# The order in which expert rows are fetched and used: bursts of sixteen of one table, or one row of each table in turn

## The chip, the cores and the metric

The kernel runs on one core of one Trainium2 chip. The time is the device time of one execution in microseconds (us). The engines are TensorE (PE), VectorE (DVE), ScalarE (ACT), GpSimd (POOL) and SyncE (SP); SBUF and PSUM are the two on-chip memories.

## The reference, cut to what matters

A block of four layers (feed-forward halves around an attention of three kinds) is followed by a block of two layers. Each of these two has a mixer and then `peer`, a layer of product keys over 16384 experts. 256 tokens, width 1024, all float32. What the change touches is the last part of `peer`:

```python
def peer(xn, w_q, keys1, keys2, u, v):
    q = (xt @ w_q).reshape(T, PEER_HEADS, 2, PEER_HALF)       # T = 256, 8 heads
    s1 = einsum('thd,nd->thn', q[:, :, 0], keys1)             # 128 keys each
    s2 = einsum('thd,nd->thn', q[:, :, 1], keys2)
    v1, i1 = top_k(s1, 16)
    v2, i2 = top_k(s2, 16)
    sc, ci = top_k(v1[..., :, None] + v2[..., None, :], 16)   # of 256 sums
    experts = i1[ci // 16] * 128 + i2[ci % 16]                # 16 per token and head
    gates = softmax(sc)
    hb = gelu(einsum('tkd,td->tk', u[experts], xt))           # k: 8 heads x 16 picks
    return einsum('tk,tkd->td', gates * hb, v[experts])
```

So every token reads 128 rows of 1024 numbers from table u, takes the dot product of each with its own vector, and sums 128 rows of table v with the coefficients that come out.

## The kernel before

One program runs all six layers. Only the two `peer` phases are touched, and in them only what follows the key scores.

**Steps.** The tokens lie on the 128 partitions, in two halves. A half and a head make a step: `STEPS` = 16 steps, step s being half s // 8 and head s % 8. A step has 16 picks per token (`BURST` = 16), hence 16 rows of u and 16 rows of v. A "row" of the program is one fetch of 128 table rows, one per partition: a tile of 128 x 1024 f32, 524 kB. A layer fetches 512 of them.

**The ring.** The tiles land in a ring of `ROWSLOTS` = 20 slots, 4 in `deep_ring` and 16 in `wide_ring`. `ROWS` is the fetch order, and `row_at` gives row k the slot k % 20. GpSimd issues all the fetches (`gather`, L2605 to L2622; the page records them at L2619) in that order, each an indirect DMA whose row numbers come from `pk_idx`. Before fetch k it waits until row k - 20 has been used, by the semaphore `row_used` (VectorE) or `row_mixed` (PE), whichever `ROW_AFTER` names; before the first u row of a step it also waits for the last pick stage of that step (`pick_stage`).

**The order.** `GATHERS` (L78 to L81) lists bursts: u of step 0, then u of step s and v of step s - 1 for s = 1 to 15, then v of step 15. Each burst is the 16 rows of one table and step.

**Who uses the rows.** VectorE does all dots (`dot`, L2446): the row times the token vectors, which lie in PSUM (`pair[1 + t]`), with the product written back over the row and the sum into `pk_dot`; a second, short instruction reads the sum out. Of the v rows, the eight with even n are added by VectorE (`accumulate`, L2486): `row_sum` (`pair[3]`, PSUM) += coefficient x row; in the last two steps the sum is kept in `resid` (SBUF) instead. The eight with odd n go through PE (L1348, four matmuls each, with a diagonal matrix that ScalarE makes at L1705), which adds them in two other PSUM banks.

**VectorE's own order.** Beside dot n of step s (0 < s < 14) stands pick stage n of step s + 2 (`pick_stage`, L2371 to L2426: 15 stages, two rounds of MAX8, FIND_INDEX8 and MATCH_REPLACE8 on the 128 scores of each half key, the same on the 256 sums, then the arithmetic that makes `pk_idx`). After dot 3 comes `reciprocal` of the step before, after dot 5 its `coefficients` (L2461), which wait for the gelu on ScalarE (L1696). After dot 15 comes `accumulate(s - 1)`, eight instructions in a row:

```python
                    if s > 0:
                        accumulate(s - 1)
                    if s == PK_HEADS:
                        fold(0)
                        add_mixed(0)
```

`fold` adds `row_sum` to `resid` at the end of each half, and `add_mixed` adds PE's sum.

Of the kernel before, what the change touches and what calls it, by code (L numbers as in the profile page):

```python
# [21 lines left out]
ALU = mybir.AluOpType  # L22
# [6 lines left out]
TT = TOK // P  # L29
# [23 lines left out]
PK_HEADS, NKEYS, TOPK = 8, 128, 16  # L53
# [14 lines left out]
BURST = 16  # L68
STEPS = TT * PK_HEADS
PICK_STAGES = 15  # L70


def on_tensor(step):

    return range(1, BURST, 2)


GATHERS = [("u", 0)]  # L78
for _step in range(1, STEPS):
    GATHERS += [("u", _step), ("v", _step - 1)]  # L80
GATHERS += [("v", STEPS - 1)]  # L81


def count_rows():

    used, mixed, after = 0, 0, {}
    for table, step in GATHERS:
        for n in range(BURST):
            if table == "v" and n in on_tensor(step):
                mixed += 1  # L90
                after[table, step, n] = ("row_mixed", mixed)
            else:
                used += 1
                after[table, step, n] = ("row_used", used)
    return used, mixed, after


ROWS_USED, ROWS_MIXED, ROW_AFTER = count_rows()
ROWS = [(table, step, n) for table, step in GATHERS for n in range(BURST)]
ROW_NUMBER = {row: k for k, row in enumerate(ROWS)}  # L100


# [52 lines left out]
def mix_before(turn):  # L155
# [28 lines left out]
                 mixed=4, mixed_read=4),  # L184
# [25 lines left out]
def build(nc, A, out, stop=None):  # L210
    phases = plan()[:stop]
    ctx = ExitStack()
    with ctx:
# [11 lines left out]
        resid = sb("resid", [P, TT, D])  # L225
# [18 lines left out]
        def cut(at, *shape):  # L244
# [111 lines left out]
        pk_coef = sb("pk_coef", [P, 2, BURST])  # L356
# [225 lines left out]
        wide_dmas, n = [], [0] * GSLOTS  # L582
# [1132 lines left out]
        def _(dve):  # L1715
            V = nc.vector
# [713 lines left out]
            def product_keys(ph):  # L2430
                i, at = ph.i, ph.at
# [32 lines left out]

                def accumulate(s):
                    t = s // PK_HEADS
                    for n in range(BURST):
                        if n in on_tensor(s):
                            continue
                        dve.wait_ge(S["coef"], STEPS * i + s + 1)  # L2470
                        row = ROW_NUMBER["v", s, n]
                        await_row(dve, ph, row)
                        coef = pk_coef[:, s % 2, n:n + 1]
                        if s % PK_HEADS == 0 and n == 0:
                            if t == 0:
                                dve.wait_ge(S["key_scores_read"], PK_HEADS * (i + 1))
                            else:
                                dve.wait_ge(S["rows_folded"], TT * i + 1)
                            V.tensor_scalar(row_sum[:], row_at(ph, row), coef, None,
                                            ALU.mult).then_inc(S["row_used"], 1)  # L2480
                            continue
# [3 lines left out]
                        total = resid[:, t] if s >= STEPS - 2 else row_sum[:]  # L2485
                        V.scalar_tensor_tensor(out=total, in0=row_at(ph, row), scalar=coef, in1=total,  # L2486
                                               op0=ALU.mult, op1=ALU.add).then_inc(S["row_used"], 1)
# [28 lines left out]
                split_head(5)  # L2516
                pick(1, 7, PICK_STAGES)
                split_head(6)
                for s in range(STEPS):
                    for n in range(BURST):  # L2520
# [3 lines left out]
                        if s == 0 and n >= BURST // 2:  # L2524
                            pick(2, 2 * n - BURST, min(2 * n - BURST + 2, PICK_STAGES))
                        if 0 < s < STEPS - 2 and n < PICK_STAGES:
                            pick_stage(ph, s + 2, n)
                        if s > 0 and n == 3:
                            reciprocal(s - 1)
                        if s > 0 and n == 5:  # L2530
                            coefficients(s - 1)
                    if s == STEPS - 1:
                        fold(1)
                    if s > 0:
                        accumulate(s - 1)
                    if s == PK_HEADS:
                        fold(0)
                        add_mixed(0)
                reciprocal(STEPS - 1)
                coefficients(STEPS - 1)  # L2540
                accumulate(STEPS - 1)
                add_mixed(1)
            for ph in phases:
                {"norm": norm, "norm_split": norm_split, "norm_final": norm, "ffn": ffn, "sb": stick_breaking,
# [154 lines left out]
```

## Time and profile before

| | |
|---|---|
| median of three runs | 3919.18 us (3918.96 to 3920.58) |
| the profiled execution | 3916.44 us |
| its span | 3914.7 us |
| granted TensorE clock, mean | 0.89 |
| PE, VectorE, ScalarE, GpSimd busy | 76%, 69%, 31%, 27% |
| bytes moved | 940.74 MB, 547.19 of them by GpSimd's queue |

The profile comes from one execution, and its parts are read against that execution's span. In its table of slices each digit is the busy share in tenths; a busy share is not yet a bound, since an engine can be busy in one stage and idle in another. Names such as `wide_ring<-in_peer_u,pk_idx` are out<-in. In a list of waits, "issue" is time in which the engine waited for nothing that the profile shows, and "remote" a wait that it can't put to another engine's instruction. The first `peer` phase fetches rows from about 2227 to 2977 us of the span, the second from about 3155 to 3905.

### The profile page before, as it was taken

The numbers are of one execution on the slowest core, as the hardware profiler recorded it, in microseconds if no ns is written. First come the engines' busy times: TensorE is split into PE (matmuls) and PEld (weight loads), VectorE is DVE, ScalarE is ACT, GpSimd is POOL, SyncE is SP. The second block draws the span as 40 slices with busy tenths as digits, with TensorE's granted clock in tenths as the row PEclk, the third lists the DMA queues.
The fourth block names the chain that finished last, engine by engine and source line by source line (L and its number), as shares of the span: only waits on it lengthen the run. The fifth ranks groups of instructions, "written<-read, shape, count | busy, mean of one in ns | idle before, by whom it ended". The sixth has DMA issues, their size and how long they took to land.

```text
span 3914.7 us, 41030 instructions
## 1 busy us (share of the span) xinstructions
PE 2983.6 (76%) x14720; PEld 2203.6 (56%) x14720; DVE 2697.0 (69%) x4716; ACT 1231.4 (31%) x1807; POOL 1054.3 (27%) x1133
## 2 busy tenths in 40 slices
PE   8999999999999999999999943433338964433344
PEld 7897888968886688897886721111114661111111
DVE  6655676666765667664664687778774587778786
ACT  5444444344442444444442311111111231111110
POOL 2000000000000000000000266666663056666665
PEclk9999999999999999999999967776769987677678
DMA  6634565435554355562563499999998279999998
GB/s 213 207 121 147 192 199 191 169 113 194 190 182 147 129 169 191 193 231 76 167 210 114 152 350 359 362 365 369 366 360 312 81 268 360 365 363 366 364 373 329
DMA packets 413639, 940.74 MB, mean 240 GB/s; under 512 B 24688, under 2 KB 209552, under 8 KB 413472
## 3 DMA queue, kind: packets, MB, share of 16 engines
q0 software_dynamic: 150800, 547.19, 37.0%
q1 hardware_dynamic: 260784, 389.57, 29.6%
q8 instruction: 96, 1.57, 0.2%
q10 hardware_dynamic: 1888, 1.84, 0.1%
q14 instruction: 71, 0.58, 0.0%
HBM read 937.45 MB, written 1.05 MB: 240 GB/s over the span
## 4 chain that ended last, share of the span: by engine, by line
PE 55%; DVE 30%; issue 5%; another core or an unknown queue 4%; DMA 2%; POOL 2%; ACT 1%; DVEq 0%; SPq 0%; POOLq 0%; ACTq 0%
DVE wide_ring L2446 11%; PE pair L937 8%; PE pair L944 8%; DVE pair L2486 7%; PE pair L706 5%; PE pair L708 5%; PE pair L707 5%; PE pair L779 4%; PE pair L942 4%; PE pair L939 4%; PE pair L800 4%; DVE deep_ring L2446 3%; PE pair L787 1%; DMA wide_ring<-in_ffn_w_gate_up 1%
## 5 line engine op out<-in xcount | busy, mean ns | idle before, releaser
L1348 PE MATMUL pair<-wide_ring,arena 128*128 128x512 f32 x816 | 443.7, 691 | 654.0 <-issue 376.6
L1727 DVE TENSOR_TENSOR wide_lo<-wide_ring,wide_hi 128x2048 fp32r<-128x2048 f32 x228 | 522.5, 2292 | 401.1 <-ACT wide_hi L1443 396.7
L1348 PEld LDWEIGHTS pair<-wide_ring,arena 128*128 128x128 f32 x816 | 170.2, 220 | 925.8 <-issue 790.9
L2598 POOL TENSOR_TENSOR small<-small,minus_half 128x2 f32<-128x2 f32 (+2 forms) x29 | 25.2, 869 | 2321.3 <-DVE small L1877 1673.3
L1443 ACT ACTIVATE wide_hi<-wide_ring 128x2048 fp32r<-128x2048 f32 x228 | 434.6, 1911 | 483.6 <-DMA wide_ring<-in_ffn_w_gate_up 323.0
L937 PE MATMUL pair<-x_both,wide_hi 128*128 128x512 f32 x1344 | 533.0, 397 | 1.6 <-DVE wide_lo L1727 1.1
L944 PE MATMUL pair<-x_both,wide_hi 128*128 128x512 f32 x1344 | 531.6, 396 | 0.0
L2446 DVE CUSTOM_DVE_ANT_0 wide_ring<-wide_ring,pair 128x1024 f32<-128x1024 f32 x408 | 490.7, 1210 | 19.3 <-issue 18.8
L2619 POOL DMA_INDIRECT wide_ring<-in_peer_v,pk_idx x408 | 394.5, 967 | 232.4 <-issue 101.1
L2619 POOL DMA_INDIRECT wide_ring<-in_peer_u,pk_idx x408 | 392.5, 962 | 164.2 <-issue 95.2
L942 PE MATMUL pair<-x_both,wide_lo 128*128 128x256 f32 x1344 | 374.2, 278 | 0.0
L939 PE MATMUL pair<-x_both,wide_lo 128*128 128x256 f32 x1344 | 372.8, 277 | 0.0
L1705 ACT ACTIVATE arena<-ident,pk_coef 128x128 f32<-128x128 f32 x256 | 78.3, 388 | 795.0 <-remote 570.0
L942 PEld LDWEIGHTS pair<-x_both,wide_lo 128*128 128x128 f32 x1344 | 252.3, 188 | 61.1
L939 PEld LDWEIGHTS pair<-x_both,wide_lo 128*128 128x128 f32 x1344 | 252.7, 188 | 56.6
L937 PEld LDWEIGHTS pair<-x_both,wide_hi 128*128 128x128 f32 x1344 | 255.1, 190 | 10.1 <-issue 8.0
L1348 PE MATMUL pair<-deep_ring,arena 128*128 128x512 f32 x208 | 114.7, 692 | 180.5 <-issue 80.5
L944 PEld LDWEIGHTS pair<-x_both,wide_hi 128*128 128x128 f32 x1344 | 251.9, 187 | 0.0
L706 PE MATMUL pair<-deep_hi,hid_hi 128*128 128x512 f32 x640 | 249.3, 390 | 0.0
L708 PE MATMUL pair<-deep_hi,hid_lo 128*128 128x512 f32 x640 | 249.0, 389 | 0.0
L707 PE MATMUL pair<-deep_lo,hid_hi 128*128 128x512 f32 x640 | 249.0, 389 | 0.0
L2486 DVE SCALAR_TENSOR_TENSOR pair<-wide_ring,pk_coef,pair 128x1024 f32<-128x1024 f32 x176 | 226.8, 1288 | 30.7 <-issue 6.2
(349 smaller groups left out, 5751.6 us busy)
## 6 DMA issues: line engine op xcount, KB each, us to landing
wide_ring<-in_ffn_w_gate_up SPq DMA_DIRECT2D x174, 1024.0 KB, 9.6
deep_ring<-in_ffn_w_down SPq DMA_DIRECT2D x88, 1024.0 KB, 4.9
wide_ring<-in_sb_w_qkv SPq DMA_DIRECT2D x12, 2048.0 KB, 12.6
wide_ring<-in_w_in SPq DMA_DIRECT2D x12, 2048.0 KB, 9.7
wide_ring<-in_peer_w_q SPq DMA_DIRECT2D x8, 2048.0 KB, 13.9
wide_ring<-in_moba_w_qkv SPq DMA_DIRECT2D x6, 2048.0 KB, 12.3
deep_ring<-in_sb_w_o SPq DMA_DIRECT2D x8, 1024.0 KB, 7.5
deep_ring<-in_w_out SPq DMA_DIRECT2D x8, 1024.0 KB, 7.6
```

The lines of the kernel that those rows point to most:

```text
L706: mm(o, w[0], x[0], start=start, stop=False, skip_group_check=True)
L707: mm(o, w[0], x[1], start=False, stop=False, skip_group_check=True)
L708: return mm(o, w[1], x[0], start=False, stop=stop, skip_group_check=True)
L937: mm(o[:, 0:2 * TOK], hi, both, start=k == 0, stop=False, skip_group_check=True)
L939: mm(o[:, 0:TOK], lo, x_hi[:, k], start=False, stop=False, skip_group_check=True)
L942: mm(o[:, 0:TOK], lo, x_hi[:, k], start=False, stop=False, skip_group_check=True)
L944: ins = mm(o[:, 0:2 * TOK], hi, both, start=False, stop=k == KT - 1, skip_group_check=True)
L1348: ins = mm(acc[t][h][:, :], pk_diag[:, s % 2, k], row_at(ph, row)[:, h * 512:(h + 1) * 512], start=first, stop=last, skip_group_check=True)
L1727: V.tensor_tensor(wide_lo[:, split_at(ph, j)], half_panel(ph, wide_ring[:, slot], j), wide_hi[:, split_at(ph, j)].bitcast(F32), ALU.subtra ...
L2446: V.tensor_tensor_reduce(out=row_at(ph, row), in0=row_at(ph, row), in1=pair[1 + s // PK_HEADS][:], scale=1.0, scalar=0.0, op0=ALU.mult, op ...
L2486: V.scalar_tensor_tensor(out=total, in0=row_at(ph, row), scalar=coef, in1=total, op0=ALU.mult, op1=ALU.add).then_inc(S["row_used"], 1)
L2619: G.indirect_dma_start(row_at(ph, k), None, tables[table], bass.IndirectOffsetOnAxis(ap=pk_idx[:, s, n:n + 1], axis=0)).then_inc(row_in[sl ...
```

## The change

The order of the rows is another. `ROWS` now begins with 24 rows of u (`U_LEAD`), then takes one row of u and one of v in turn, and ends with the 24 rows of v that are left. Beside u row (s + 1, n + 8) stands v row (s, n). VectorE goes through the same list: `accumulate` now handles one row, and it waits by semaphore for the row that VectorE accumulated before it. The pick stages, `reciprocal` and `coefficients` stand beside the same dots as before. `fold` and `add_mixed` are placed by rows of v; `add_mixed(0)` comes three rows of v later than `fold(0)`. PE and ScalarE follow `ROWS` with unchanged code; their instructions and their order are the same as before.

```diff
-GATHERS = [("u", 0)]
-for _step in range(1, STEPS):
-    GATHERS += [("u", _step), ("v", _step - 1)]
-GATHERS += [("v", STEPS - 1)]
+U_LEAD = BURST + BURST // 2
+
+
+def order_of_rows():
+
+    def row(table, k):
+        return table, k // BURST, k % BURST
+    count = STEPS * BURST
+    rows = [row("u", k) for k in range(U_LEAD)]
+    for k in range(count):
+        if k + U_LEAD < count:
+            rows.append(row("u", k + U_LEAD))
+        rows.append(row("v", k))
+    return rows
+
+
+ROWS = order_of_rows()
...
-                def accumulate(s):
+                def accumulate(s, n):
...
-                        dve.wait_ge(S["row_used"], ROWS_USED * i + ROW_AFTER["v", s, n][1] - 1)
-                        if s == STEPS - 2:
-                            dve.wait_ge(S["rows_folded"], TT * (i + 1))
...
+                    before = ("v", s, n - 2) if n > 0 else ("v", s - 1, BURST - 2)
+                    dve.wait_ge(S["row_used"], ROWS_USED * i + ROW_AFTER[before][1])
+                    if s == STEPS - 2 and n == 0:
+                        dve.wait_ge(S["rows_folded"], TT * (i + 1))
...
-                for s in range(STEPS):
-                    for n in range(BURST):
+                for table, s, n in ROWS:
+                    if table == "u":
                         if s == 0 and n == 3:
                             split_head(7)
                         dot(s, n)
...
-                    if s == STEPS - 1:
+                        beside_dot(s, n)
+                        continue
+                    if s == STEPS - 2 and n == 0:
                         fold(1)
-                    if s > 0:
-                        accumulate(s - 1)
-                    if s == PK_HEADS:
+                    if s == STEPS - 2 and n == BURST - 4:
+                        reciprocal(STEPS - 1)
+                    if s == STEPS - 1 and n == 0:
+                        coefficients(STEPS - 1)
+                    if n not in on_tensor(s):
+                        accumulate(s, n)
+                    if s == PK_HEADS - 1 and n == BURST - 1:
                         fold(0)
+                    if s == PK_HEADS and n == 2:
                         add_mixed(0)
-                reciprocal(STEPS - 1)
-                coefficients(STEPS - 1)
-                accumulate(STEPS - 1)
                 add_mixed(1)
```

VectorE before, at the end of a step in mid-layer (ISA is a dot, `ISA pk_dot` the short read of its sum; L2424 and L2426 are the last two pick stages, L2380 is the first of the next):

```order
L2446 ISA wide_ring,pk_dot<-wide_ring,pair 128x1024
L2446 ISA pk_dot 128x1
L2426 SCALAR_TENSOR_TENSOR pk_idx<-pk_e 128x16
L2446 ISA wide_ring,pk_dot<-wide_ring,pair 128x1024
L2446 ISA pk_dot 128x1
L2486 SCALAR_TENSOR_TENSOR pair<-deep_ring,pk_coef,pair 128x1024 x2
L2486 SCALAR_TENSOR_TENSOR pair<-wide_ring,pk_coef,pair 128x1024 x6
L2446 ISA wide_ring,pk_dot<-wide_ring,pair 128x1024
L2446 ISA pk_dot 128x1
L2380 MAX pk_v<-arena 128x8 x2
L2446 ISA wide_ring,pk_dot<-wide_ring,pair 128x1024
```

VectorE after, over the same pick stages (the dot is now L2458, the accumulation L2497):

```order
L2458 ISA wide_ring,pk_dot<-wide_ring,pair 128x1024
L2458 ISA pk_dot 128x1
L2426 CAST pk_ab<-pk_abu 128x32
L2497 SCALAR_TENSOR_TENSOR pair<-wide_ring,pk_coef,pair 128x1024
L2458 ISA wide_ring,pk_dot<-wide_ring,pair 128x1024
L2458 ISA pk_dot 128x1
L2429 TENSOR_TENSOR arena<-pk_ab,iota 128x512
L2458 ISA deep_ring,pk_dot<-deep_ring,pair 128x1024
L2458 ISA pk_dot 128x1
L2433 TENSOR_TENSOR arena<-arena,pk_if 128x512
L2497 SCALAR_TENSOR_TENSOR pair<-deep_ring,pk_coef,pair 128x1024
L2458 ISA deep_ring,pk_dot<-deep_ring,pair 128x1024
```

The eight accumulations that stood together stand one by one, each behind every second dot.

GpSimd before, at the first fetches of the layer that wait for a slot to come free (in brackets the semaphores that a fetch waits for):

```order
L2619 DMA deep_ring<-in_peer_u,pk_idx 128x1024 [waits row_used] x4
L2619 DMA wide_ring<-in_peer_u,pk_idx 128x1024 [waits row_used] x8
L2619 DMA wide_ring<-in_peer_v,pk_idx 128x1024 [waits row_used] x8
L2619 DMA deep_ring<-in_peer_v,pk_idx 128x1024 [waits row_used] x4
L2619 DMA wide_ring<-in_peer_v,pk_idx 128x1024 [waits row_used] x4
L2619 DMA wide_ring<-in_peer_u,pk_idx 128x1024 [waits row_used,pick_stage]
L2619 DMA wide_ring<-in_peer_u,pk_idx 128x1024 [waits row_used] x4
```

GpSimd after, at the same place (the fetch is now L2637):

```order
L2637 DMA deep_ring<-in_peer_u,pk_idx 128x1024 [waits row_used] x4
L2637 DMA wide_ring<-in_peer_u,pk_idx 128x1024 [waits row_used]
L2637 DMA wide_ring<-in_peer_v,pk_idx 128x1024 [waits row_used]
L2637 DMA wide_ring<-in_peer_u,pk_idx 128x1024 [waits row_used]
L2637 DMA wide_ring<-in_peer_v,pk_idx 128x1024 [waits row_used]
L2637 DMA wide_ring<-in_peer_u,pk_idx 128x1024 [waits row_used]
```

Where twelve fetches of u and sixteen of v followed one another, fetches of u and v alternate from the 25th on. The count of instructions on GpSimd, PE and ScalarE is the same; VectorE has 4830 instead of 4844, the 14 fewer being semaphore waits.

## Rows read from the trace of the kernel before

**Rows 1.** The table of slices: three of its lines of tenths in 40 slices.
```profile
PE   8999999999999999999999943433338964433344
DVE  6655676666765667664664687778774587778786
...
DMA  6634565435554355562563499999998279999998
```

**Rows 2.** Windows of ten and eleven steps; columns are named in the first row.
```profile
core 0: us, PE busy (x) PEld busy (x) DVE busy (x) ACT busy (x) POOL busy (x), PEclk, DMA share, GB/s
2343.00:2805.00 462.00, 177.72 (x325) 69.44 (x324) 363.00 (x773) 58.11 (x130) 301.34 (x320) 0.70 0.96 363
3271.00:3778.00 507.00, 191.80 (x356) 74.66 (x355) 399.01 (x850) 63.93 (x143) 331.02 (x352) 0.70 0.96 364
```

**Rows 3.** VectorE's waits in the ten steps: us in total, times, longest us.
```profile
DVE pk_sc L2407 <- remote: 28.8, 7, 6.9
DVE pk_neg L2402 <- remote: 12.2, 8, 2.5
DVE pk_sc L2400 <- remote: 11.6, 4, 6.0
DVE pk_sc L2400 <- issue: 7.1, 2, 6.0
DVE pk_sc L2407 <- issue: 6.5, 2, 5.6
```

**Rows 4.** Lines of GpSimd in the ten steps: busy, mean ns, idle before.
```profile
L2619 POOL DMA_INDIRECT wide_ring<-in_peer_v,pk_idx x128 | 121.1, 946 | 76.3 <-issue 29.6 <-remote 28.0 <-DVE pk_dot L2446 18.7
L2619 POOL DMA_INDIRECT wide_ring<-in_peer_u,pk_idx x128 | 119.9, 936 | 49.1 <-issue 27.3 <-DVE pk_dot L2446 11.0 <-DVE arena L2421 5.5
```

**Rows 5.** Windows inside two steps, in the last burst with dots, and behind it.
```profile
2437.00:2443.00 6.00, 4.66 (x12) 1.82 (x10) 6.00 (x15) 1.77 (x3) 3.91 (x5) 1.00 0.65 199
2443.00:2457.00 14.00, 5.83 (x10) 2.05 (x8) 13.20 (x18) 0.31 (x1) 9.49 (x11) 0.88 0.93 337
2457.00:2483.00 26.00, 8.68 (x16) 3.52 (x16) 16.79 (x46) 3.73 (x9) 16.77 (x18) 0.61 1.03 410
2483.00:2489.00 6.00, 3.28 (x7) 1.17 (x7) 5.72 (x15) 1.77 (x3) 3.75 (x4) 1.00 0.70 222
2489.00:2503.00 14.00, 4.95 (x11) 1.54 (x9) 13.20 (x18) 0.31 (x1) 9.58 (x10) 0.94 0.96 336
2503.00:2528.00 25.00, 7.96 (x13) 3.42 (x14) 16.94 (x46) 3.73 (x9) 16.86 (x18) 0.56 1.02 408
2880.00:2906.00 26.00, 15.26 (x28) 5.84 (x28) 22.77 (x35) 2.75 (x9) 19.59 (x22) 0.73 1.03 409
2934.00:2975.00 41.00, 30.14 (x57) 11.10 (x58) 20.11 (x18) 3.67 (x12) 30.68 (x27) 0.91 0.98 374
```

**Rows 6.** Timeline of VectorE, then of GpSimd, around one wait.
```profile
2528.25 0.43 DVE L2407 MAX8 pk_sc<-arena 128x8 f32<-128x256 f32 x1 [6.94 <-remote]
...
2524.37 0.94 POOL L2619 DMA_INDIRECT deep_ring<-in_peer_v,pk_idx  x1 [0.30 <-issue]
2529.90 0.94 POOL L2619 DMA_INDIRECT deep_ring<-in_peer_v,pk_idx  x1 [4.59 <-DVE pk_dot L2446]
```

**Rows 7.** Lines of VectorE in the ten steps, then one burst from its timeline.
```profile
L2446 DVE CUSTOM_DVE_ANT_0 wide_ring<-wide_ring,pair 128x1024 f32<-128x1024 f32 x128 | 154.8, 1209 | 6.3 <-issue 6.3
L2486 DVE SCALAR_TENSOR_TENSOR pair<-wide_ring,pk_coef,pair 128x1024 f32<-128x1024 f32 x63 | 81.2, 1289 | 8.4
...
2498.32 8.40 DVE L2486 SCALAR_TENSOR_TENSOR pair<-wide_ring,pk_coef,pair 128x1024 f32<-128x1024 f32 x6
```

**Rows 8.** Lines of ScalarE and of PE in the ten steps.
```profile
L1696 ACT ACT_TABLE_LOAD x10 | 12.8, 1283 | 0.2
L1696 ACT ACTIVATE pk_gelu<-pk_dot,small 128x16 f32<-128x16 f32 x10 | 3.1, 308 | 94.4 <-DVE pk_dot L2446 86.4 <-issue 8.0
...
L1348 PE MATMUL pair<-wide_ring,arena 128*128 128x512 f32 x261 | 142.8, 699 | 226.3 <-issue 126.2 <-ACT arena L1705 45.4 <-remote 29.2
```

More of the change, by code:

```diff
@@ L75, in on_tensor @@
     return range(1, BURST, 2)
-GATHERS = [("u", 0)]
-for _step in range(1, STEPS):
-    GATHERS += [("u", _step), ("v", _step - 1)]
-GATHERS += [("v", STEPS - 1)]
+U_LEAD = BURST + BURST // 2
[10 more added lines that the diff above has]
+ROWS = order_of_rows()
 def count_rows():
     used, mixed, after = 0, 0, {}
-    for table, step in GATHERS:
-        for n in range(BURST):
[L89 to L94, printed above, removed]
+    for table, step, n in ROWS:
+        if table == "v" and n in on_tensor(step):
+            mixed += 1
+            after[table, step, n] = ("row_mixed", mixed)
+        else:
+            used += 1
+            after[table, step, n] = ("row_used", used)
     return used, mixed, after
 ROWS_USED, ROWS_MIXED, ROW_AFTER = count_rows()
-ROWS = [(table, step, n) for table, step in GATHERS for n in range(BURST)]
 ROW_NUMBER = {row: k for k, row in enumerate(ROWS)}
@@ L2463, in coefficients @@
                                            ).then_inc(S["coef"], 1)
-                def accumulate(s):
+                def accumulate(s, n):
                     t = s // PK_HEADS
[L2467 to L2481, printed above, removed]
-                        dve.wait_ge(S["row_used"], ROWS_USED * i + ROW_AFTER["v", s, n][1] - 1)
-                        if s == STEPS - 2:
-                            dve.wait_ge(S["rows_folded"], TT * (i + 1))
-                        total = resid[:, t] if s >= STEPS - 2 else row_sum[:]
-                        V.scalar_tensor_tensor(out=total, in0=row_at(ph, row), scalar=coef, in1=total,
-                                               op0=ALU.mult, op1=ALU.add).then_inc(S["row_used"], 1)
@@ new lines, in accumulate @@
+                    dve.wait_ge(S["coef"], STEPS * i + s + 1)
+                    row = ROW_NUMBER["v", s, n]
+                    await_row(dve, ph, row)
+                    coef = pk_coef[:, s % 2, n:n + 1]
+                    if s % PK_HEADS == 0 and n == 0:
+                        if t == 0:
+                            dve.wait_ge(S["key_scores_read"], PK_HEADS * (i + 1))
+                        else:
+                            dve.wait_ge(S["rows_folded"], TT * i + 1)
+                        V.tensor_scalar(row_sum[:], row_at(ph, row), coef, None,
+                                        ALU.mult).then_inc(S["row_used"], 1)
+                        return
@@ new lines, in accumulate @@
+                    before = ("v", s, n - 2) if n > 0 else ("v", s - 1, BURST - 2)
+                    dve.wait_ge(S["row_used"], ROWS_USED * i + ROW_AFTER[before][1])
+                    if s == STEPS - 2 and n == 0:
+                        dve.wait_ge(S["rows_folded"], TT * (i + 1))
+                    total = resid[:, t] if s >= STEPS - 2 else row_sum[:]
+                    V.scalar_tensor_tensor(out=total, in0=row_at(ph, row), scalar=coef, in1=total,
+                                           op0=ALU.mult, op1=ALU.add).then_inc(S["row_used"], 1)
@@ L2518, in product_keys, with beside_dot @@
                 split_head(6)
-                for s in range(STEPS):
-                    for n in range(BURST):
+                def beside_dot(s, n):
+                    if s == 0 and n >= BURST // 2:
+                        pick(2, 2 * n - BURST, min(2 * n - BURST + 2, PICK_STAGES))
+                    if 0 < s < STEPS - 2 and n < PICK_STAGES:
+                        pick_stage(ph, s + 2, n)
+                    if s > 0 and n == 3:
+                        reciprocal(s - 1)
+                    if s > 0 and n == 5:
+                        coefficients(s - 1)
+                for table, s, n in ROWS:
+                    if table == "u":
                         if s == 0 and n == 3:
@@ L2523, in product_keys @@
                         dot(s, n)
[L2524 to L2531, printed above, removed]
-                    if s == STEPS - 1:
-                        fold(1)
-                    if s > 0:
-                        accumulate(s - 1)
-                    if s == PK_HEADS:
+                        beside_dot(s, n)
+                        continue
+                    if s == STEPS - 2 and n == 0:
+                        fold(1)
+                    if s == STEPS - 2 and n == BURST - 4:
[5 more added lines that the diff above has]
+                    if s == PK_HEADS - 1 and n == BURST - 1:
                         fold(0)
+                    if s == PK_HEADS and n == 2:
                         add_mixed(0)
-                reciprocal(STEPS - 1)
-                coefficients(STEPS - 1)
-                accumulate(STEPS - 1)
                 add_mixed(1)
```

## The prediction

> **What bounds the kernel now.** The table of slices comes first [rows 1]. In the two product-key layers (slices 24 to 31 and 33 to 40, of 97.9 us each) the transfer engines' digit is 9 except at the edges and VectorE's mostly 7 or 8, while PE sinks to 3 or 4. So either the fetching or VectorE sets the end there. The two stretches are some 1500 us of the span, and the change touches nothing outside them.
>
> Next, the windows over ten whole steps of the first layer and eleven of the second [rows 2]. I cut them where VectorE resumes after the wait that comes once in each step. 462 by ten and 507 by eleven are **46.1 us per step**. VectorE is busy 363.0 / 10 = 36.3 us of it, the transfer engines 0.96 of it, at 363 GB/s. One row is 128 x 1024 f32, 0.524 MB; a step moves 32 rows, 16.8 MB.
>
> Who waits? VectorE's waits [rows 3] name no transfer at all: it never stands for a row of the tables. They stand at the pick instructions L2400, L2402 and L2407, with no recorded releaser: these first five rows are 66.2 us, 6.6 per step. GpSimd, in turn, waits for slots that VectorE has not freed [rows 4]: `DVE pk_dot` ends 18.7 and 11.0 us of the idle time before its fetches, "remote" 28.0.
>
> The stretches inside two steps show how the two go together [rows 5]. A step has three parts: about 6 us at 199 GB/s, 14 us at 337, and 26 us at 410. The next step repeats it (222, 336, 408). 410 is the ceiling: the last burst without picks runs at 409 as well. At 410 a step would take 16.8 / 0.410 = 40.9 us, so 5.2 us of each step are lost to the first two parts. VectorE is busy 6.0 of 6 and 13.2 of 14 us in them, but only 16.8 of 26 in the fast part. The idle time lies in the last third of the fast part: after dot 7 VectorE stands 6.9 us before MAX8 L2407, whose only wait is for its own, finished predecessor; GpSimd issues three more fetches, finds no free slot and stands for 4.6 us; the transfers drain [rows 6]. That is the 6 us part. I can't name the cause of this stall; I can only say where it comes: after some 17 us of VectorE's work, or 46 of its instructions, at 410 GB/s.
>
> **The change part by part.** It removes no fetch, no dot, no accumulation and no pick: the same 77 recorded VectorE instructions per step (773 in ten [rows 2]), in another order. Cost of the work itself: 0.
>
> *The middle part.* It runs at 337 because slots come free at the pace of a burst of dots. That pace is (36.3 - 8 x 1.289) / 16 = 1.62 us per row [rows 2, 7], the picks included, while a fetch is issued every 0.936 + 0.30 = 1.24 us [rows 4, 6] and lands every 0.524 / 0.410 = 1.28. With one u and one v in turn, VectorE frees two rows with a dot and half an accumulation: 36.3 / 32 = 1.13 us per row, less than 1.24. GpSimd is then never held after the drain, and the 14 us part joins the fast one. The stall stays, and it now comes after 6 + 26 us instead of 46. Such a cycle moves 6 x 199 + 26 x 410 = 11.85 MB, 22.6 rows in 32 us, or 45.3 us per 32 rows: **0.8 us less than 46.1**. The gain is small because the stall with its drain now comes 1.4 times per step. Steps 1 to 13 have picks beside them or just ahead, in two layers: 26 x 0.8 = 21 us.
>
> *The head.* A lead of 24 u rows instead of 32: eight rows leave VectorE's pace of 1.62 for 1.42 (45.3 / 32): 1.6 us per layer, 3 in all.
>
> *The tail.* The last rows are v alone, 32 of them before, 24 now. They run at 374 GB/s, 1.40 us per row [rows 5]; at best eight of them go to 1.28: 1 us per layer, 2 in all.
>
> *The accumulations.* In a burst one takes 8.40 / 6 = 1.40 us against 1.289 busy [rows 7]: 0.11 is the wait for the one ahead. Now a dot stands between. Below, that is 0; above, 0.11 x 8 = 0.9 us per step of VectorE's time, 23 us in all. I take 0, since in the forecast VectorE is not what paces the cycle, and because the pair of waits ahead of the instruction stays.
>
> *The waits that move.* The indices of step s+2 are complete when dot (s, 14) is done. The first fetch that reads them stood 50 places of the fetch order behind that dot and stands 36 behind it now; GpSimd leads by at most 20, so 16 are spare: 0. Between the last dot of a step and its coefficients lie 6 dots and 3 accumulations, about 14 us, where before there were 6 dots and a burst, about 21; the gelu needs its table load and itself, 1.283 + 0.308 us [rows 8]: 0. `add_mixed(0)` may now wait for PE's last row of the half, four matmuls of 0.70 us [rows 8]: 0 to 2.8 once per layer; I take 0. On GpSimd's queue each fetch of v now waits in turn for VectorE and for PE; PE uses a row as it lands, and its slot is asked for 20 places later: 0.
>
> **Sum:** 21 + 3 + 2 = 26 us less. The profiled execution took 3916.4, so 3890 on its own scale. The median of the runs shown is 3919.2, 2.8 above it: **3893**.
>
> **A rule against it.** The row says that 410 GB/s is held for 26 us in each step, and 363 and 364 on the mean in the two layers [rows 2, 5]. The Trainium skill (DMA: Bandwidth & Descriptors, section Bandwidth) says that for transfers from HBM into SBUF the HBM side binds, at about 358 GB/s per core. By that rule there would be nothing to gain, and the time stays 3919. It also gives 425 for a core that streams alone, which is the side on which the 410 lies. The sum goes by the row.
>
> **The rivals.**
> - *Nothing moves* (3919). The mean over a step could be what is limited, in whatever state of the order; 363 and 364 in two layers speak for that, and so does that VectorE does not wait for rows, which means the change mends an unevenness that the ring of 20 already takes up. Against it: the 14 us at 337 follow the pace of the dots. Chance 0.17.
> - *The stalls go* (3784). If they come from dense picks at full rate, spreading the picks over 41 us instead of 26 thins them. VectorE's 36.3 us fit under the 40.9 of the transfers: 5.2 x 26 = 135 us less. In the last burst without picks [rows 5] VectorE is busy 22.8 of 26 us at 409 GB/s, so full rate and a working VectorE go together where there are no picks. Against it: the picks are no fewer per row. Half of that would be 3851. Chance 0.20.
> - *The stall eats VectorE* (slower). If a stall follows each 17 us of VectorE's work at full rate, a cycle of 32 us holds 6.0 + 16.8 = 22.8 us of it. A step then takes 36.3 / 22.8 x 32 = 50.9 us: 4.8 x 26 = 125 us more, 4044. The place is VectorE's queue, at whichever pick stands there. It decides as soon as VectorE is idle for more than 6.4 of 32 us, since 22.6 rows need 25.6; at 7.5 it would be 47.4 us per step and 3953. Now it is idle 9.2 of 26. For the forecast the stall must go by instructions rather than by time: 46 now stand in 16.8 us of work, where all the dense picks are; spread evenly (77 in 36.3) 46 are 21.7 us of work, which leaves 4.3 idle. Chance 0.27.
>
> **How the numbers follow.** Forecast 0.36. Less than 0.2% (8 us) is about what a measurement of this kernel tells from no change. Faster is the forecast and the second rival, 0.56; same is the first, 0.17; slower the third, 0.27. As both signs hold much: the forecast's own range is 3865 (with the 23 us of the accumulations) to 3910. The whole one is 3800 to 3985: it takes in most of the second rival and the nearer half of the third, and leaves out some 0.17.
>
> **What would show it.** Right: windows in mid-layer without a stretch near 337 that lasts 14 us; a mean of 368 to 371 GB/s; waits without a releaser in front of picks, spaced some 32 us. The third rival: the same spacing, a mean under 355, VectorE busy under 0.77. The second: long stretches at 410 and VectorE waiting for rows. The first: 363 again, in whatever pattern. I am wrong altogether if VectorE's busy time per step changes by more than 1 us, or if GpSimd waits for `pick_stage` or `row_mixed`.

## The result, and the profile after

| | before | after |
|---|---|---|
| median | 3919.07 us (3917.55 to 3920.58, 4 runs) | 3894.98 us (3891.74 to 3897.63, 4 runs) |
| the profiled execution | 3916.44 us | 3891.74 us |
| its span | 3914.7 us | 3890.0 us |

The ratio is 0.9942, with a 95% interval of 0.9929 to 0.9955: 24 us faster, where 26 was forecast. One run of the kernel before, among those of the second chip below, took 5490.91 us at a granted clock of 0.549 and not 0.89, and is left out of every comparison. Of the profile after, the lines that answer to [rows 1], and one of PE:

```profile
DVE  6655676666765667664664687878775588778785
...
DMA  6634555535554456462563299999998279999998
...
L1360 PE MATMUL pair<-wide_ring,arena 128*128 128x512 f32 x824 | 548.5, 811 | 558.2 <-DMA wide_ring<-in_peer_v,pk_idx 220.7
```

The line of PE before:

```profile
L1348 PE MATMUL pair<-wide_ring,arena 128*128 128x512 f32 x816 | 443.7, 691 | 654.0 <-issue 376.6
```

In the two product-key layers (slices 24 to 31 and 33 to 40) the digits of the transfers are the same as before; the difference lies inside the steps. So I cut twelve whole steps of each layer, from the first dot of step 2 to the first dot of step 14. The same cut of the kernel before (columns as in [rows 2]):

```profile
2320.40:2875.50 555.10, 211.35 (x384) 82.07 (x384) 435.35 (x929) 69.73 (x156) 362.12 (x385) 0.71 0.96 363
3248.40:3801.50 553.10, 208.06 (x384) 80.81 (x384) 435.21 (x929) 69.74 (x156) 361.09 (x385) 0.70 0.96 365
```

And after:

```profile
core 0: us, PE busy (x) PEld busy (x) DVE busy (x) ACT busy (x) POOL busy (x), PEclk, DMA share, GB/s
2314.20:2852.10 537.90, 260.69 (x382) 92.17 (x383) 427.67 (x928) 69.73 (x156) 362.62 (x383) 0.71 0.97 372
3226.10:3765.50 539.40, 253.71 (x383) 90.27 (x384) 427.15 (x928) 69.74 (x156) 364.11 (x384) 0.72 0.97 372
```

A step took 46.3 and 46.1 us and takes 44.8 and 45.0: 1.3 less, at 372 GB/s instead of 363 and 365. VectorE's busy time fell a little, from 36.3 to 35.6 us per step. In all, the twelve steps gain 17.2 us in the first layer and 13.7 in the second. The rest of each layer is its two ends, steps 0 and 1 and what follows the first dot of step 14; here those of the first layer, before:

```profile
2246.30:2320.40 74.10, 37.12 (x180) 25.57 (x178) 63.76 (x146) 14.60 (x26) 49.19 (x50) 0.72 0.93 338
2875.50:2977.10 101.60, 49.09 (x92) 18.01 (x93) 70.37 (x96) 9.18 (x30) 69.09 (x68) 0.76 0.95 369
```

and after:

```profile
2247.20:2314.20 67.00, 33.69 (x174) 23.85 (x172) 58.41 (x141) 14.18 (x25) 44.96 (x46) 0.73 0.94 342
2852.10:2962.30 110.20, 64.84 (x103) 20.88 (x101) 73.65 (x101) 9.49 (x31) 75.59 (x75) 0.82 0.96 370
```

74.1 + 101.6 = 175.7 became 67.0 + 110.2 = 177.2; in the second layer 175.2 became 178.9. (The first part is shorter and the last longer because the rows of v begin eight rows earlier.) The ends give back 1.5 and 3.7 us. Over both layers that is 30.9 - 5.2 = 25.7 us, against 24.7 by which the spans differ.

VectorE's waits after, which answer to [rows 3] (stretch 2343 to 2780, picks are now L2392 to L2438):

```profile
DVE pk_if L2405 <- remote: 22.6, 6, 4.8
DVE pk_v L2400 <- remote: 12.8, 4, 6.9
DVE pk_v L2400 <- issue: 11.6, 2, 6.9
DVE pk_i L2403 <- remote: 7.7, 3, 3.5
```

Still no transfer is named, and still nothing is recorded that releases these waits. They only stand at other picks, L2400 to L2405 (MAX8 of the second round, FIND_INDEX8, the first CAST). That no transfer is named is weak evidence by itself, since most landings are missing from this trace (last section). But these picks wait by their code for the pick stage before them alone, which had ended, and ahead of all dots VectorE stood for only 10 us in this stretch. And the parts of a step, as in [rows 5]:

```profile
2379.00:2388.00 9.00, 7.45 (x12) 3.00 (x12) 9.00 (x22) 5.50 (x12) 6.86 (x8) 0.74 0.79 263
2388.00:2418.00 30.00, 15.07 (x20) 4.87 (x20) 21.82 (x47) 0.31 (x1) 20.56 (x23) 0.77 1.02 407
2463.00:2475.00 12.00, 3.61 (x5) 1.55 (x6) 11.94 (x29) 3.73 (x9) 8.50 (x10) 0.50 0.84 275
2475.00:2511.00 36.00, 16.95 (x29) 5.84 (x27) 27.89 (x61) 2.08 (x4) 25.76 (x27) 0.83 1.03 411
```

In these two steps 9 and 12 us run at 263 and 275 GB/s, then 30 and 36 us at 407 and 411. The middle part at 337, which was 14 us long, is gone as a part of its own, but the slow part ahead of the fast one is longer than the 6 us that I had put down for it.

### The profile page after: what moved, and what is told of

It reads as the page before. It is cut to its first block, busy times and chain, and to the rows that moved or that the text cites. A ratio compares the mean times of both kernels' runs of the same rounds, so it can differ in the third digit from the quotient of the medians.

```text
span 3890.0 us, 41016 instructions
## 1 busy us (share of the span) xinstructions
PE 3105.2 (80%) x14720; PEld 2225.6 (57%) x14720; DVE 2676.8 (69%) x4716; ACT 1230.8 (32%) x1807; POOL 1063.2 (27%) x1133
## 4 chain that ended last, share of the span: by engine, by line
PE 55%; DVE 27%; issue 8%; another core or an unknown queue 4%; DMA 3%; POOL 1%; ACT 1%; SPq 0%; DVEq 0%; POOLq 0%; ACTq 0%
DVE wide_ring L2458 8%; PE pair L949 8%; PE pair L956 8%; DVE pair L2497 7%; PE pair L718 5%; PE pair L720 5%; PE pair L719 5%; PE pair L791 4%; PE pair L954 4%; PE pair L951 4%; PE pair L812 4%; DVE deep_ring L2458 2%; DMA wide_ring<-in_ffn_w_gate_up 2%; PE pair L799 1%
## 5 line engine op out<-in xcount | busy, mean ns | idle before, releaser
L1360 PE MATMUL pair<-wide_ring,arena 128*128 128x512 f32 x824 | 548.5, 811 | 558.2 <-DMA wide_ring<-in_peer_v,pk_idx 220.7
L1360 PEld LDWEIGHTS pair<-wide_ring,arena 128*128 128x128 f32 x824 | 190.6, 250 | 914.2 <-issue 711.1
L2458 DVE CUSTOM_DVE_ANT_0 wide_ring<-wide_ring,pair 128x1024 f32<-128x1024 f32 x404 | 486.2, 1209 | 13.5 <-issue 12.4
L2637 POOL DMA_INDIRECT wide_ring<-in_peer_u,pk_idx x404 | 396.8, 982 | 188.8 <-issue 112.5
L2637 POOL DMA_INDIRECT wide_ring<-in_peer_v,pk_idx x412 | 398.0, 966 | 176.1 <-issue 118.7
L2497 DVE SCALAR_TENSOR_TENSOR pair<-wide_ring,pk_coef,pair 128x1024 f32<-128x1024 f32 x178 | 227.1, 1276 | 26.5 <-remote 24.8
L1360 PE MATMUL pair<-deep_ring,arena 128*128 128x512 f32 x200 | 135.1, 813 | 121.9 <-DMA deep_ring<-in_peer_v,pk_idx 61.6
```

Source lines behind the costliest of these rows:

```text
L1360: ins = mm(acc[t][h][:, :], pk_diag[:, s % 2, k], row_at(ph, row)[:, h * 512:(h + 1) * 512], start=first, stop=last, skip_group_check=True)
L2458: V.tensor_tensor_reduce(out=row_at(ph, row), in0=row_at(ph, row), in1=pair[1 + s // PK_HEADS][:], scale=1.0, scalar=0.0, op0=ALU.mult, op ...
L2637: G.indirect_dma_start(row_at(ph, k), None, tables[table], bass.IndirectOffsetOnAxis(ap=pk_idx[:, s, n:n + 1], axis=0)).then_inc(row_in[sl ...
```

## The experiments

Two theories stood at the start. **A, VectorE's own time:** it never waits for a row, so a step is its work and its stalls; the gain is that an accumulation no longer stands behind another, where it took 1.40 us and not 1.28. **B, the fetches' pace:** the gain is that slots come free evenly, so that the transfers spend more of the time at 410 GB/s. A third, **C**, was that the shorter lead brings it.

**Turns of four.** One line of `order_of_rows`:

```diff
-    for k in range(count):
-        if k + U_LEAD < count:
-            rows.append(row("u", k + U_LEAD))
-        rows.append(row("v", k))
+    for k in range(0, count, 4):
+        rows += [row("u", j + U_LEAD) for j in range(k, k + 4) if j + U_LEAD < count]
+        rows += [row("v", j) for j in range(k, k + 4)]
```

> The changed order with turns of four: 24 u rows ahead, then four of u and four of v. VectorE then has two accumulations next to one another in each turn, 4 such neighbours per step where the kernel before has 7 and the change none. Theory A (VectorE's own time is the step's time: it never waits for a row, and an accumulation right behind another costs some 0.24 us more than one behind a dot): 4/7 of the 1.3 us per step is lost again, 0.74 x 26 = 19 us, so about 3914 us, and small gaps of VectorE of some 0.6 us per step. Theory B (the fetches' pace: what counted is that slots come free evenly): a ring of 20 evens out four rows, so 3895 within 4.

Measured: 3774.90 us (10 runs), and the kernel before beside it 3775.55 (31 runs): 0.9999 [0.9989, 1.0008].

**Turns of eight**, the same with 8 for 4.

> Turns of eight. 6 neighbouring accumulations per step. Theory A: 6/7 of the gain is lost, 1.1 x 26 = 29 us, capped by the kernel before: about 3919 to 3923. Theory B: eight dots at 1.6 us per row hold GpSimd for a few rows only, so at most a third of the gain is lost: 3895 to 3903.

Measured: 3776.48 us, 1.0000 [0.9991, 1.0010].

**A lead of 32.** `U_LEAD = 2 * BURST`.

> The change with a lead of 32 u rows, as long as before, and then one row of each in turn. Theory A and theory B alike: nothing in mid-layer changes, so 3895 within 5, the ends aside. Theory C (the shorter lead is what brought the gain): 3915 to 3919.

Measured: 3775.20 us, 0.9998 [0.9989, 1.0008].

**Twelve of sixteen v rows on PE.**

```diff
+ON_VECTOR = (0, 4, 8, 12)
...
-    return range(1, BURST, 2)
+    return [n for n in range(BURST) if n not in ON_VECTOR]
```

> The change with 12 of a step's 16 v rows on PE instead of 8; VectorE adds 4. Its work falls by 4 x 1.29 = 5.2 us per step, to 30.5. Theory A: 30.5 plus stalls of 9 is 39.7, under the 40.9 that the transfers need at 410 GB/s, so the step becomes 41 to 42 us and VectorE begins to wait for rows: 28 x 3.5 = about 95 us less, 3800 us (3785 to 3830). Theory B: the stalls still drain the transfers once per 45 us, 3880 to 3895. PE at 2.8 to 3.2 us per row needs 34 to 38 us per step; if it is held, 3850 or more.

Measured: 3775.62 us, 1.0001 [0.9992, 1.0011].

All four expectations missed, under every theory: on this chip the kernel before itself takes 3775.55 us, 144 less than in the runs of the result. Twelve steps of the kernel with turns of four show why (this row and the two below it in the columns of [rows 2]):

```profile
2306.60:2792.40 485.80, 276.27 (x373) 105.74 (x374) 430.12 (x929) 69.72 (x156) 364.58 (x386) 0.72 1.03 409
```

with a lead of 32:

```profile
2299.50:2780.20 480.70, 267.29 (x371) 85.02 (x372) 431.44 (x929) 70.04 (x157) 361.41 (x383) 0.77 1.03 408
```

and with twelve v rows on PE:

```profile
2305.20:2793.30 488.10, 327.11 (x563) 120.27 (x562) 377.41 (x881) 84.08 (x205) 365.30 (x388) 0.85 1.03 409
```

408 to 409 GB/s from end to end, 40.1 to 40.7 us per step. VectorE's busy time in the last of the three is 377 us instead of 430, and the kernel's time is the same. The two largest groups of VectorE's waits with turns of four, in the stretch 2350 to 2700:

```profile
DVE wide_ring L2457 <- DMA wide_ring<-in_peer_u,pk_idx: 23.6, 24, 1.3
DVE pair L2496 <- DMA wide_ring<-in_peer_v,pk_idx: 10.2, 16, 1.3
```

Now transfers end them, and there is no wait without a releaser at a pick. The stalls are not there, and the transfers' 1.28 us per row set the time in all the orders tried. So this group tells nothing of A and B where the stalls are; it shows what the kernels cost where they are not.

**The two kernels themselves, and two loads on VectorE**, on a second chip. (Each group of runs was on one chip at one time, with the kernel before beside it, so the chip and the occasion are not told apart. Which chip the result was taken on is not known.)

> The kernel before, unchanged, for a profile beside the other experiments: in the runs of the first experiments it took 3775.6 us, not 3919. Theory S (VectorE's stalls without a releaser are a condition of the chip or of the run, not of the order, and without them the transfers' 1.28 us per row is the bound): 3775, 409 to 410 GB/s throughout mid-layer, 40.9 us per step, no waits without a releaser at the picks. If the stalls are there: 3919.

Measured: 3927.72 us (10 runs), the kernel before beside it 3927.00. The stalls are there:

```profile
2320.70:2878.10 557.40, 210.40 (x384) 81.11 (x384) 435.25 (x928) 69.82 (x156) 363.36 (x385) 0.70 0.96 361
```

> The changed kernel, unchanged, likewise. Theory S: where the kernel before takes 3775 this one does too, within 0.1%, with VectorE waiting for rows; where it takes 3919 this one takes 3895.

Measured: 3900.88 us (4 runs), 0.9930 [0.9913, 0.9946], 26 us less: the result holds here too.

```profile
2314.10:2857.10 543.00, 267.49 (x384) 93.10 (x384) 428.75 (x928) 69.74 (x156) 364.02 (x385) 0.68 0.98 371
3236.70:3779.50 542.80, 257.58 (x385) 90.34 (x384) 429.30 (x928) 69.75 (x156) 362.62 (x384) 0.71 0.98 370
```

45.2 us per step against 46.5, close to the 44.9 and 46.2 of the result.

**More instructions on VectorE:**

```diff
+                    for q in range(2):
+                        V.tensor_copy(spare[:, 2 * n + q:2 * n + q + 1], minus_half[:, 0:1])
```

> The change with two more instructions of 128x1 behind each dot, on a tile that nothing reads: 32 per step (77 to 109), about 0.07 us each, 2.2 us of VectorE's time. Without stalls: VectorE needs 38 of 40.9 us, the transfers bound, no change from the changed kernel. With stalls: theory N (a stall comes after so many VectorE instructions at full rate): stalls grow by 109/77, 9 to 12.7 us per step, and with the 2.2 the step becomes 51 us: 150 us more than the changed kernel. Theory T (it comes after so much time): 2.2 us per step, 60 us more.

Measured: 3916.84 us (4 runs), 0.9968 [0.9952, 0.9983], 16 more than the changed kernel. Both expectations, 150 and 60 us more, are far too high.

```profile
2322.20:2866.70 544.50, 256.85 (x384) 90.78 (x384) 455.70 (x1313) 69.68 (x157) 363.81 (x384) 0.72 0.98 370
3247.20:3795.50 548.30, 266.40 (x388) 92.33 (x386) 455.51 (x1314) 69.73 (x156) 364.15 (x385) 0.70 0.98 369
```

VectorE is busy 455.6 us instead of 429, 2.2 more per step, and the step is 0.1 and 0.5 us longer. Theory A asks for the whole 2.2. VectorE's idle time shrank instead, from 9.5 to 7.4 us per step in the first layer, and it came in many short waits: in the stretch 2343 to 2780 none is longer than 2.0 us, where the changed kernel on this chip has waits of 6.6. So the idle time does not grow with the number of instructions either.

**Fewer.** This kernel leaves out the picks of steps 3 to 15; they fetch again the rows that step 2 picked:

```diff
+                if s > 2:
+                    if n < PICK_STAGES - 1:
+                        return
...
+                    V.scalar_tensor_tensor(out=pk_idx[:, s], in0=pk_e[:, 0], scalar=float(NKEYS),
+                                           in1=pk_e[:, 1], op0=ALU.mult, op1=ALU.add
+                                           ).then_inc(S["pick_stage"], PICK_STAGES)
```

> The change without the pick stages of steps 3 to 15: those steps fetch the rows that step 2 picked, and their gates are left as they are, so this part of the computation is left out. VectorE's work falls by some 9 us per step, its instructions from 77 to about 43. Without stalls: the transfers bound, so the time stays that of the changed kernel within 0.2%, which would show that VectorE's work has no part in it. With stalls: 41 us per step and 3790 if the stalls need the picks, 3850 or more if they don't.

Measured: 3885.62 us (2 runs), 0.9893 [0.9873, 0.9913], 15 less than the changed kernel: over 3850, as expected if the stalls don't need the picks. That the same table rows are read again is a second difference, which no run takes apart.

```profile
2306.80:2835.30 528.50, 289.96 (x377) 91.09 (x376) 357.25 (x521) 70.13 (x157) 351.96 (x375) 0.71 0.97 373
```

VectorE's busy time is 357 us, 6.0 less per step, and the step is 1.2 less. In both directions a microsecond of VectorE's work is worth 0.05 to 0.2 us of a step. Over the whole kernel it is 0.2 and 0.1: 73 us more of VectorE's work cost 16 us, and 153 less gained 15. **Theory A falls.**

When does a stall come? Here are stretches, picked by eye, from where the transfers reach 410 GB/s to where VectorE first stops. In the kernel before, from the trace that the result was compared with:

```profile
2458.00:2472.00 14.00, 0.00 (x0) 0.00 (x0) 13.58 (x38) 0.00 (x0) 10.50 (x12) 0.50 1.03 413
2505.00:2521.00 16.00, 0.96 (x1) 0.50 (x2) 14.99 (x44) 1.85 (x7) 12.04 (x14) 0.50 1.02 412
2544.00:2562.00 18.00, 0.00 (x0) 0.00 (x0) 16.56 (x37) 0.00 (x0) 13.42 (x16) 0.64 1.02 409
```

in the changed one, from the trace of the result:

```profile
2475.00:2498.00 23.00, 13.41 (x25) 4.67 (x23) 23.00 (x49) 2.08 (x4) 17.51 (x19) 0.91 1.03 412
2524.00:2545.00 21.00, 10.17 (x17) 3.19 (x16) 20.72 (x42) 0.31 (x1) 16.12 (x17) 0.82 1.03 411
2390.00:2406.00 16.00, 7.27 (x11) 2.34 (x10) 16.00 (x33) 0.31 (x1) 12.08 (x13) 0.84 1.03 412
```

with more instructions, on the second chip:

```profile
2529.00:2545.00 16.00, 9.58 (x20) 3.66 (x19) 15.80 (x43) 1.77 (x3) 12.34 (x13) 0.93 1.02 413
2574.00:2588.00 14.00, 10.24 (x17) 3.49 (x15) 14.00 (x36) 1.88 (x4) 10.79 (x11) 0.77 1.03 415
```

and without picks, to where GpSimd stops:

```profile
2465.00:2522.00 57.00, 32.35 (x46) 10.58 (x47) 40.99 (x59) 7.90 (x17) 39.50 (x42) 0.82 1.03 410
```

The first three groups last 14 to 18, 16 to 23 and 14 to 16 us, with 37 to 44, 33 to 49 and 36 to 43 VectorE instructions (the x behind DVE). Neither number decides between a count and a time. The last stretch does not fit one fixed time: it lasts 57 us with 59 instructions. But there it is another engine that stops, GpSimd, ahead of a fetch, so its count of VectorE's instructions is not comparable either. That a stall goes by instructions, as the forecast needed it, is not shown. The stop without picks:

```profile
2517.92 0.94 POOL L2645 DMA_INDIRECT wide_ring<-in_peer_u,pk_idx  x1 [0.30 <-issue]
2526.03 0.94 POOL L2645 DMA_INDIRECT wide_ring<-in_peer_v,pk_idx  x1 [7.17 <-remote]
```

7.17 us with no releaser; PE had freed the slot that this fetch takes 23 us before it was issued. There are 25 gaps of over 3 us between GpSimd's fetches in the two layers, and ten times exactly 52 fetches lie between one and the next (8 to 56 the other times). A stall without a releaser is thus not a thing of the picks, nor of VectorE.

**Slower fetches.** If the stalls need 410 GB/s, then fetches that are issued a little apart should avoid them.

```diff
+                    if k >= ROWSLOTS and k % 2 == 0:
+                        chain(G.memset(spare[:, k % 4:k % 4 + 1], 0.0))
```

> The change with a small memset, and the wait for it, ahead of every second fetch on GpSimd's queue, so that a fetch is issued every 1.33 to 1.40 us instead of 1.24. The transfers then never come to 410 GB/s, but run at 375 to 394. Theory P (the stalls without a releaser come only after a stretch at 410 GB/s, on whichever engine): where the kernel before has the stalls, they go, and a step takes 43 to 44.5 us instead of 45.2: 20 to 55 us less than the changed kernel. If the stalls stay in spite of it, the slower issue adds to them: 3900 or more. On a chip without stalls: 32 x 0.1 us per step more, 3800 to 3840.

Measured on a third chip, where the kernel before takes 3775.15: 3773.39 us, 0.9998 [0.9988, 1.0008]. Its twelve steps, then a memset and the fetch behind it:

```profile
2303.50:2788.80 485.30, 265.46 (x375) 84.88 (x376) 432.14 (x930) 70.05 (x157) 374.58 (x564) 0.78 1.02 406
2450.39 0.11 POOL L2639 MEMSET spare<- 128x1 f32 x1
2450.77 0.94 POOL L2640 DMA_INDIRECT wide_ring<-in_peer_u,pk_idx  x1 [0.27 <-POOL spare L2639]
```

A fetch with a memset ahead comes 0.08 us later, 0.04 on the mean: 1.28, just the pace of the transfers. It costs nothing, where 3800 to 3840 us was expected without stalls, and it slows nothing: it says nothing of the stalls.

**Turns of eight again**, in the same group.

> Turns of eight, where the stalls are there. Theory A (VectorE's own time) has fallen with the run of 32 more instructions and the one without picks; what is left is the cycle of the transfers: how much of the time they run at 410. With turns of eight VectorE frees eight slots at some 1.5 us each, then four accumulations with eight rows of PE beside them: half the gain or more, 3901 to 3914 where the kernel before takes 3927 and the changed one 3901. As much as the changed kernel (within 4) would say that the ring evens out eight rows and that only bursts of sixteen cost.

Measured: 3774.33 us, 0.9998 [0.9988, 1.0007]. No stalls on this chip, so no answer.

**The changed kernel again**, on a fourth chip.

> The changed kernel once more, beside the run with slower fetches. So far two chips gave 3775 for the kernel before (409 GB/s throughout, no wait without a releaser on VectorE) and two gave 3919 to 3927. Where the kernel before takes 3775, this takes 3775 within 4, since only the transfers' 1.28 us per row counts there; where it takes 3927, this takes 3901.

Measured: 3774.77 us (10 runs), the kernel before beside it 3774.55: 1.0001 [0.9991, 1.0010]. As expected for a chip without stalls; here are its twelve steps and the largest group of VectorE's waits from 2343 to 2780:

```profile
2306.10:2792.10 486.00, 269.99 (x375) 86.87 (x376) 432.04 (x929) 70.05 (x157) 364.34 (x386) 0.77 1.03 409
DVE wide_ring L2458 <- DMA wide_ring<-in_peer_u,pk_idx: 37.8, 55, 1.4
```

**Still slower fetches.**

```diff
+                    if k >= ROWSLOTS:
+                        chain(G.memset(spare[:], 0.0))
```

> The change with a memset of 128x64 and the wait for it ahead of every fetch after the first 20: 0.08 us for the smaller one in the first trial, so some 0.12 more and a fetch every 1.36 us, 385 GB/s. Where there are no stalls: 1.36 instead of 1.28 for some 480 rows, two layers: 77 us more, 3850. Where there are: theory P (they come only after a stretch at 410 GB/s) gives 43.5 to 44 us per step and no waits without a releaser, 30 to 50 us less than the changed kernel, 3850 to 3870; if they come at 385 GB/s too, 3900 to 3950.

Measured: 3893.15 us, 1.0315 [1.0298, 1.0333].

```profile
2307.40:2837.80 530.40, 301.82 (x378) 95.42 (x378) 434.99 (x929) 70.05 (x157) 421.27 (x753) 0.67 0.99 372
2450.30 0.17 POOL L2639 MEMSET spare<- 128x64 f32 x1
2450.73 0.94 POOL L2640 DMA_INDIRECT wide_ring<-in_peer_v,pk_idx  x1 [0.27 <-POOL spare L2639]
2451.68 0.17 POOL L2639 MEMSET spare<- 128x64 f32 x1
```

A fetch every 1.38 us instead of 1.24, 44.2 us per step. That is 3.7 us more per step than on this chip without the memset, 119 in all, where 77 was expected: a fetch came 0.14 us later and not 0.12, and 0.10 over the transfers' 1.28 for 2 x 492 fetches is 98; the rest was not followed. On a chip without stalls this is pure loss; whether it would avoid them where they are was not seen, as the group met none.

## Why the prediction was right, and where it was not

The number was right to 2 us, 3895 for 3893, and that close it came by luck. The direction was right, and so was the place of the gain, the part of a step at 337 GB/s. But the terms were off: 21 us were forecast for mid-layer and 31 came, 5 less for the head and the tail and 5 more came.

- **What bounds the kernel.** Right for this profile: in a cycle a stall without a releaser lets the transfers drain, and the cycle repeats. What the prediction did not see is that this is not a property of the kernel. On three of the four chips of the experiments the same program takes 3775 us, and the traces taken there without added memsets run at 408 to 409 GB/s throughout mid-layer.
- **Cost of the work itself, 0.** Right in the count of instructions: 928 recorded on VectorE in twelve steps, before 929.
- **The middle part.** "GpSimd is then never held after the drain, and the 14 us part joins the fast one": the first half is shown. After the stall its fetches follow one another at 1.24 us:

```profile
2378.71 0.94 POOL L2637 DMA_INDIRECT deep_ring<-in_peer_u,pk_idx  x1 [4.81 <-DVE pk_dot L2458]
2379.95 0.94 POOL L2637 DMA_INDIRECT deep_ring<-in_peer_v,pk_idx  x1 [0.30 <-issue]
...
2387.41 0.93 POOL L2637 DMA_INDIRECT wide_ring<-in_peer_v,pk_idx  x1 [0.30 <-issue]
```

The second half is wrong in size. In these same 9 us the transfers are at 263 GB/s, although eight fetches are issued in them, which is the rate of 423: the transfers first have to fill again. The slow part is 9 to 12 us long, not 6. Against that, the fast stretch is 30 to 36 us long, not 26; that it is longer because the picks are no longer packed into it is my reading, not shown. The cycle of 32 us that I forecast is one of about 45, and the stall comes about once per step, not 1.4 times. Both sizes were off, in opposite directions. What came out was 1.3 us per step, where 0.8 was forecast: 31 us in the twenty-four whole steps, where 26 x 0.8 = 21 stood.
- **The accumulations, taken as 0.** VectorE's time did fall: 0.6 us per step of busy time, and the 8.4 us of idle time ahead of L2486 in ten steps [rows 7] are gone. The bound above, 23 us in all, took such time as the kernel's. The runs with more and with less work on VectorE show that a microsecond of it is worth 0.05 to 0.2, so this is an estimated 0.1 to 0.3 us of the 1.3.
- **The head and the tail, 5 us less.** Wrong in sign: 5.2 us more. The last parts ran on at 370 GB/s, and at 361 in the second layer, not at 410. In the last part of each layer VectorE now stands 2.7 to 4.1 us ahead of five accumulations, some 16 us in all and again without a recorded releaser; before, there was one such wait in the first layer and two in the second. The forecast had no stalls there.
- **The moved waits, 0.** Among VectorE's waits in mid-layer none names PE, and GpSimd's fetches follow at 1.24 us after a stall. With so many semaphore records missing this is not a strict proof.
- **The rivals.** "The stall eats VectorE" fell: VectorE is idle 9.2 us per step, before 10.0, as the stalls stayed about one step apart. "The stalls go" did not come about through the change. But it named nearly the right size for the case in which they are not there: 3784 was its time, and 3775 was measured on three chips. There "nothing moves" holds as well, for another reason than its own: the change can give nothing where the transfers are never interrupted.
- **What would show it.** The mean of 372 GB/s lies just outside the 368 to 371 asked for; the spacing of the waits was 32 us in the forecast and is about 45 over the layer: VectorE comes out of them at 2557, 2602, 2641, 2690 and 2730, 39 to 49 us apart. By its own sign the cycle was wrong, while the sum held.

What stays open: where the stalls are, whether the turn of one row or a turn of four or eight is needed, and what the lead does. All runs that could tell fell on chips without stalls. That the gain comes from a larger share of the time at 410 GB/s is read from the trace (in windows of 1 us, over 398 GB/s in 259 of the 437 us from 2343 to 2780 after, 59%, and in 233 of the 462 from 2343 to 2805 before, 50%) and from the failure of theory A; it was not shown by a run that changes that share alone. Nor is it known whether the gain exists in an execution that is not recorded (last section).

## What to carry to other kernels

Before an unevenness is mended, ask whether the wait that makes it belongs to the program. Here the kernel took 144 to 152 us more where the unexplained waits were, and they were absent on three of the four chips of the experiments, while the change was worth 24 to 26 us where they were and nothing measurable where they were not. And where an engine never waits for data, its work need not be what sets the pace: adding and removing some of it is the cheap way to find out.

## What the runs showed of the hardware

- The same program took 3919 us in the runs of the result, 3927 on the second chip of the experiments and 3775 on the three others, each within 0.3%. The traces differ in stalls without a recorded releaser; in the stretches looked at they came after 14 to 57 us at 410 GB/s.
- In the stretches looked at, VectorE stalled after 33 to 49 of its instructions at full rate, and where VectorE had little to do, GpSimd stood still, often 52 fetches after the last time. A stall ends near the moment when the transfers drain, but not by it: in the changed kernel VectorE resumed at 2641.36 and the rate fell below 400 GB/s at 2643; without picks the rate was 4 GB/s at 2524 and GpSimd resumed at 2526.03.
- Where the stalls are, the trace itself gets thin at full rate: in 12 us at 410 GB/s it holds 17 semaphore updates (changed kernel, second chip), and 163 on the fourth chip with the same kernel at the same rate. Over the whole kernel the two traces hold 16172 and 28782 semaphore updates. Up to the first fetch of a row both hold 9539; in each layer's row fetches, whose 512 fetches make 8192 updates on landing, the fourth chip's trace has them all and the second's has 2488 and 2249. The instruction records are complete in both, 41016. That may be a symptom or belong to the cause; no run tells which. It would fit an engine that is held because its own records are not written away. The Trainium skill (NOTIFIC — the notification-queue block, section 7.1 Overflow: three behaviours, one of which stalls the engine) says that the block which writes the trace's records holds back the engine rather than lose a record inside the block. The traces agree in part: the engines' instruction records are all there, but semaphore updates were lost, so something loses records as well. No run here was made without records, so this stays a candidate and is not shown; if it holds, the stalls, and with them the 24 us, belong to the recorded execution.
- 409 GB/s was the mean over 485 us (turns of four), by one core alone. The Trainium skill (DMA: Bandwidth & Descriptors, section Bandwidth) gives about 358 GB/s per core as what the HBM side allows, which it also calls the share when both cores of a pair stream, and 425 for a core that streams alone; the trace disagrees with the first as a bound here and lies at 96% of the second.
- An indirect fetch with a small memset and a wait ahead of it is issued 0.08 us later (128x1) or 0.14 (128x64), and as long as the sum stays at 1.28 us, the transfers' own pace, it costs nothing.
- PE's matmuls of a row take 811 ns instead of 691 when rows of v come one by one. PE is busy 122 us longer over the whole kernel (3105.2 us, before 2983.6), and no wait of VectorE in mid-layer names it. Why they take longer was not followed.
